# The third weight block of the out projection in buffers of its own, split before the projection begins

## The chip, the cores and the metric

The kernel runs on one core of one Trainium2 chip. The metric is device time of one execution, in microseconds, as the median of several runs. Five engines work beside each other: TensorE (PE) multiplies, VectorE (DVE), ScalarE (ACT) and GpSimd (POOL) do the elementwise work, SyncE (SP) issues the weight loads. They wait for each other by semaphores only, and each does its own instructions in the order in which they were written.

## The reference

Two decoder layers over 512 tokens of width 1024. Each layer mixes tokens (layer 0 by a gated linear unit, layer 1 by an attention with forgetting), adds cross-attention into 256 memory tokens, multiplies the joined heads by an output matrix (the out projection), adds the residual and normalises, then does a squared-ReLU MLP. All of it is float32.

```python
for layer in range(DEPTH):
    if layer < N_A_LAYERS:
        mix = chunked_sgu(zu, zv, a_w_s[layer], a_b_s[layer])   # gate
    else:
        mix = fox_attention(q, k_sh, v_sh, logcum)              # attention
    mo = memory_attention(qm, mk, mv)
    y = jnp.concatenate([mix, mo], axis=-1) @ w_o[layer]        # out projection
    x = layer_norm(DN_ALPHA * x + y, ln_g[layer, 0], ln_b[layer, 0])
    x = layer_norm(DN_ALPHA * x + sq_relu_mlp(x, w_up[layer], w_down[layer]),
                   ln_g[layer, 1], ln_b[layer, 1])
```

## The kernel before

Activations lie transposed in SBUF, 8 tiles of 128 features by 512 tokens. Every weight matrix is streamed in blocks of 128 output features (1024 x 128, 512 KB). A float32 product is made of three products of the faster type fp32r: both operands are split into a high part (a cast copy, `hi`) and the rest (`lo = whole - hi`), and TensorE adds hi*hi, hi*lo and lo*hi. So a block goes through four stations:

1. SP loads it into one of two places of `w_raw` as soon as the block two before it is split (`load`, waits for `w_split`).
2. ScalarE copies it into `w_hi`: `prepare` on that engine, the copy is line 1066. It waits until the block has landed and until TensorE no longer needs the place (`space(b)`, a count of `w_used`).
3. VectorE subtracts, `w_lo = w_raw - w_hi`: `prepare` on that engine, the subtraction is line 1462 (the helper `rest`).
4. TensorE runs 24 products (line 513) into one of two PSUM banks `proj`.

`w_hi` and `w_lo` have two places each, taken in turn, so that a block can in general be split only when TensorE has finished the block two before it. A few blocks have places of their own (`SPLIT_UNITS`, `split_hi` and `split_lo`), and for them `space` asks for nothing; for those in `EARLY_UNITS` it asks for three blocks before instead of the usual one.

The blocks are numbered through the program. The out projection has eight: 18 to 25 in layer 0 and 114 to 121 in layer 1. In the prediction, block 1 to block 8 stand for these in either layer. The first two are multiplied in pieces while the gate or the last attention step still runs (`out_start`), and are finished after it. Block 3 and block 4 are multiplied whole (512 tokens); for blocks 5 to 8 TensorE does the first 256 tokens of each, then the second 256. Blocks 7 and 8 are `SPLIT_UNITS`. Odd blocks use bank `proj0`, even ones `proj1`, and a bank is free when VectorE has added it into the residual `x32`.

What stands around that, in `out_projection`:

- VectorE adds the residual of blocks 1 and 2 (line 1665), takes a shift for the layer norm (line 1709, from a TensorE product `shift_sum` that stands after 15 of the 24 products of block 3), subtracts it from both tiles (line 1672), and for blocks 3 and 4 does a subtraction of the shift (line 1678) and an add of the bank (line 1684). For blocks 5 to 8 the subtraction is line 1691 and the add of half the tokens line 1702. Between these stand the calls of `prepare`.
- ScalarE squares each finished tile (lines 1203 and 1210) between its own calls of `prepare`.
- GpSimd sums the tiles and their squares (lines 2054 and 2064).
- TensorE reads these sums (`layer_sums`, line 813) after the first halves of blocks 5 to 8. All later work of the layer stands behind that.

The order on each engine is written out by hand; nothing is scheduled by a program.

## Time and profile before

| | us |
|---|---|
| median of 3 runs | 1207.45 |
| lowest and highest | 1206.73, 1207.56 |
| the profiled execution, its own time | 1207.21 |
| its span in the trace | 1205.5 |
| TensorE matmuls busy | 1161.2 (96%) |
| VectorE busy | 632.7 (52%) |
| ScalarE busy | 491.2 (41%) |
| GpSimd busy | 129.3 (11%) |

About 1.7 us of the profiled execution lie outside its span. TensorE is busy almost throughout, so time can be won only where it waits, or where it runs at a lower clock. The out projection of layer 0 lies at 160 to 205 us of the span, that of layer 1 at 794 to 839 us.

### The profile page before, as it was taken

The page shows a single profiled execution, that of the slowest core. Times are in us where ns is not written, and L with a number is a line of the kernel's source. Part 1 is how long each engine was busy: PE and PEld are TensorE (multiplying, and loading weights), DVE is VectorE, ACT ScalarE, POOL GpSimd, SP SyncE. Part 2 cuts the span into 40 slices and gives each one's busy share as a digit, 9 for nine tenths or more (in the row PEclk, how much of TensorE's full clock was granted, in tenths as well). Part 3 has the DMA queues.
Part 4 walks back from the last instruction along what each step waited for, and adds up shares of the span by engine and source line. Part 5 has one row for each costly group of instructions (what it writes and reads, how often), then busy time and mean ns, then how long its engine had stood idle before and what let it go on. Part 6 is the DMA issues. An engine that isn't in the chain of part 4 may idle for free.

```text
span 1205.5 us, 16763 instructions
## 1 busy us (share of the span) xinstructions
PE 1161.2 (96%) x5888; PEld 976.6 (81%) x5888; DVE 632.7 (52%) x1032; ACT 491.2 (41%) x852; POOL 129.3 (11%) x156
## 2 busy tenths in 40 slices
PE   5998999999999999999998999999999999999997
PEld 5777779888888888789877888878888888888886
DVE  4477766644332445345576777866544323445226
ACT  4445535634211333224665555635543212334120
POOL 2300025100000000023300000026200000000000
PEclk9999999999999999999998999999999999999999
DMA  7422122333323333332311122212333333333332
GB/s 219 134 70 71 53 90 86 88 89 103 105 87 104 88 101 91 105 88 73 86 35 53 54 70 62 60 53 84 93 104 90 102 104 87 88 98 93 105 105 87
DMA packets 185590, 107.22 MB, mean 89 GB/s; under 512 B 4482, under 2 KB 180162, under 8 KB 185540
## 3 DMA queue, kind: packets, MB, share of 16 engines
q1 hardware_dynamic: 180112, 99.36, 28.5%
q10 hardware_dynamic: 5428, 7.18, 1.9%
q8 instruction: 32, 0.52, 0.2%
q14 instruction: 18, 0.15, 0.0%
HBM read 104.43 MB, written 2.10 MB: 88 GB/s over the span
## 4 chain that ended last, share of the span: by engine, by line
PE 74%; DVE 4%; ACT 4%; issue 3%; POOL 1%; DMA 0%; DVEq 0%; ACTq 0%; POOLq 0%; SPq 0%
PE proj L513 59%; PE pv L513 3%; PE sc L513 2%; PE proj L846 2%; PE pv L846 2%; PE tr L846 2%; PE sc L846 2%; PE tr L561 1%; DVE w_lo L1462 1%; ACT w_hi L1066 1%; ACT x L1232 1%; ACT x_hi L1234 1%; POOL total L2054 0%; DVE split_lo L1462 0%; POOL total L2064 0%
## 5 line engine op out<-in xcount | busy, mean ns | idle before, releaser
L1462 DVE TENSOR_TENSOR w_lo<-w_raw,w_hi 128x1024 fp32r<-128x1024 f32 x173 | 219.6, 1270 | 172.3 <-ACT w_hi L1066 124.2
L513 PE MATMUL proj<-x_hi,w_hi 128*128 128x512 f32 (+1 forms) x768 | 300.5, 393 | 1.9 <-ACT relu L1097 1.0
L513 PE MATMUL proj<-x_hi,w_lo 128*128 128x512 f32 (+1 forms) x768 | 295.9, 386 | 0.0
L513 PE MATMUL proj<-x_lo,w_hi 128*128 128x512 f32 (+1 forms) x768 | 289.8, 384 | 0.0
L1066 ACT CAST w_hi<-w_raw 128x1024 fp32r<-128x1024 f32 x160 | 166.9, 1044 | 168.6 <-PE proj L513 166.9
L513 PEld LDWEIGHTS proj<-x_hi,w_hi 128*128 128x128 f32 x768 | 146.1, 190 | 28.9 <-ACT x_hi L1234 2.2
L513 PEld LDWEIGHTS proj<-x_hi,w_lo 128*128 128x128 f32 x768 | 145.8, 190 | 29.2
L513 PEld LDWEIGHTS proj<-x_lo,w_hi 128*128 128x128 f32 x768 | 143.1, 189 | 25.7
L513 PE MATMUL proj<-h_hi,w_hi 128*128 128x512 f32 (+1 forms) x384 | 146.4, 381 | 2.5 <-DVE w_lo L1462 2.5
L513 PE MATMUL proj<-h_lo,w_hi 128*128 128x512 f32 (+1 forms) x384 | 146.0, 380 | 0.0
L513 PE MATMUL proj<-h_hi,w_lo 128*128 128x512 f32 (+1 forms) x384 | 146.0, 380 | 0.0
L1755 DVE TENSOR_TENSOR h_raw<-relu 128x512 f32<-128x512 f32 x64 | 44.3, 692 | 157.7 <-ACT relu L1097 157.7
L1097 ACT ACTIVATE relu<-proj 128x512 f32<-128x512 f32 x64 | 38.2, 597 | 196.0 <-PE proj L513 196.0
L513 PEld LDWEIGHTS proj<-h_hi,w_hi 128*128 128x128 f32 x384 | 72.2, 188 | 16.8 <-DVE w_lo L1462 3.1
L513 PEld LDWEIGHTS proj<-h_lo,w_hi 128*128 128x128 f32 x384 | 72.2, 188 | 13.8
L513 PEld LDWEIGHTS proj<-h_hi,w_lo 128*128 128x128 f32 x384 | 72.2, 188 | 13.7
L1129 ACT ACTIVATE probs<-sc,neg_max 128x128 f32<-128x128 f32 (+2 forms) x64 | 33.0, 516 | 55.9 <-DVE neg_max L1521 54.9
L2005 POOL TENSOR_TENSOR x_lo<-x,x_hi 128x256 fp32r<-128x256 f32 (+1 forms) x56 | 48.5, 875 | 58.0 <-ACT x L1230 24.8
L1462 DVE TENSOR_TENSOR h_lo<-h_raw,h_hi 128x512 f32 (+1 forms) x64 | 44.3, 692 | 14.9 <-ACT h_hi L1246 14.4
L2054 POOL TENSOR_TENSOR total<-x 128x512 f32<-128x512 f32 x3 | 4.5, 1499 | 440.9 <-DVE x L1672 440.9
L513 PE MATMUL proj<-mix_hi,w_hi 128*128 128x256 f32 (+1 forms) x128 | 45.8, 358 | 2.5 <-DVE w_lo L1462 2.2
L1665 DVE SCALAR_TENSOR_TENSOR x<-x,proj 128x512 f32 (+1 forms) x22 | 15.1, 687 | 61.0 <-PE proj L513 61.0
(344 smaller groups left out, 1805.4 us busy)
## 6 DMA issues: line engine op xcount, KB each, us to landing
w_raw<-in_w_up SPq DMA_DIRECT2D x64, 512.0 KB, 4.0
w_raw<-in_w_down SPq DMA_DIRECT2D x64, 512.0 KB, 3.6
w_raw<-in_w_o SPq DMA_DIRECT2D x16, 512.0 KB, 3.6
w_raw<-in_a_w_in SPq DMA_DIRECT2D x14, 512.0 KB, 3.8
w_raw<-in_kv_w SPq DMA_DIRECT2D x12, 512.0 KB, 3.9
w_raw<-in_mem_w_kv SPq DMA_DIRECT2D x8, 512.0 KB, 4.9
w_raw<-in_b_w_q SPq DMA_DIRECT2D x8, 512.0 KB, 3.6
x_nat<-in_x ACTq DMA_DIRECT2D x2, 1024.0 KB, 11.4
```

Source lines behind the costliest of these rows:

```text
L513: last = pe.matmul(target, lhs, rhs, start=start and n == 0, stop=stop and n == len(terms) - 1)
L561: last = pe.transpose(tr[t.slot][0:n, at:at + rows], piece, ident[0:rows, 0:rows])
L846: last = pe.matmul(rows_of[t][n][:, :], lhs, rhs, start=False, stop=stop and m == 2, skip_group_check=True)
L1066: act.copy(weights(b)[0], w_raw[:, b.slot]).then_inc(w_hi_ready, 1)
L1097: act.activation(target, proj[g.slot][:, 0:target.shape[-1]], function).then_inc(proj_free[g.slot], 1)
L1129: act.activation(probs[:, u % 2, 0:n], sc[u % 2][:, 0:n], ACT.Exp, bias=neg_max[:, u:u + 1], accum_out=row_sum[:, u:u + 1]).then_inc(exp_d ...
L1232: act.activation(x32[:, k, own], x32[:, k, own], ACT.Identity, **gain).then_inc(fin_ready, 1)
L1234: act.copy(x_hi[:, k, own], x32[:, k, own]).then_inc(x_hi_ready, 1)
L1462: return dve.tensor_tensor(target, whole, hi.bitcast(F32), ALU.subtract)
L1665: dve.scalar_tensor_tensor(out=tile if target is None else target, in0=tile, scalar=ALPHA if first else 1.0, in1=proj[g.slot][:, :], op0=A ...
L1755: dve.tensor_tensor(raw, wide, wide, ALU.mult).then_inc(relu_sq, 1)
L2005: pool.tensor_tensor(x_lo[:, k, own], x32[:, k, own], x_hi[:, k, own].bitcast(F32), ALU.subtract).then_inc(x_ready, 1)
```

## The change

Block 3 of both layers (20 and 116, the new `LEAD_UNITS`) gets buffers of its own, `lead_hi` and `lead_lo`, in the 8 KB of `qm`, the memory queries, which are no longer read by then. Its `prepare` moves ahead: in layer 0 behind the loop of the gate, in layer 1 into the last attention step, on ScalarE and VectorE before the last `attended`. Inside `out_projection` every later `prepare` moves up by one: block 4 stands where block 3 stood, and so on, and the last of them (block 8) stands before the first half of block 5 is squared or added. Block 5 (22, 118) may be split as soon as block 1 is finished.

```diff
-    EARLY_UNITS = [26, 27, 28, 29, 30, 31, 92, 93, 94, 122, 123, 124, 125]
+    LEAD_UNITS = [20, 116]
+    EARLY_UNITS = LEAD_UNITS + [22, 118, 26, 27, 28, 29, 30, 31, 92, 93, 94, 122, 123, 124, 125]
...
+        lead_hi = put("lead_hi", [P, KT, P], F32R, top + 32 * K1)
+        lead_lo = put("lead_lo", [P, KT, P], F32R, top + 36 * K1)
...
+            if b.trip is None and b.base in LEAD_UNITS:
+                return lead_hi[:, :, :], lead_lo[:, :, :]
             return w_hi[:, b.slot], w_lo[:, b.slot]
...
+                if late is not None:
+                    prepare(Pos(LEAD_UNITS[1]))
...
             def out_projection(layer):
                 b, g, n = B_WO[layer], G_WO[layer], 2 * layer
-                prepare(Pos(b + 2))
+                prepare(Pos(b + 3))
                 shift_source(n, g)
-                prepare(Pos(b + 3))
+                prepare(Pos(b + 4))
                 for j in range(4):
                     if j >= 2:
-                        prepare(Pos(b + j + 2))
+                        prepare(Pos(b + j + 3))
                     squares(n, Pos(j), Pos(g + j))
...
                 for j in range(4, KT):
-                    if j < 6:
-                        prepare(Pos(b + j + 2))
+                    if j == 4:
+                        prepare(Pos(b + 7))
                     part_squares(n, j, 0)
...
+            prepare(Pos(LEAD_UNITS[0]))
             act.wait_ge(sgu_ready, 2 * PAIRS)
...
                 for j in range(2):
                     residual(n, Pos(b + j), Pos(g + j), Pos(j))
-                    prepare(Pos(b + j + 2))
+                for j in range(2):
+                    prepare(Pos(b + j + 3))
                 take_shift(n)
                 shift_tiles(n, g)
                 for j in range(2, 4):
                     shifted_residual(n, Pos(b + j), Pos(g + j), Pos(j))
-                    prepare(Pos(b + j + 2))
+                    prepare(Pos(b + j + 3))
...
                 for j in range(4, 6):
                     pre_shift(n, j)
-                    prepare(Pos(b + j + 2))
+                    if j == 4:
+                        prepare(Pos(b + 7))
                     part_residual(n, b + j, j, 0)
```

What this does to the order, first on ScalarE in layer 1, from the end of the last attention step (`pb_hi`, `mix_hi`) to the first square of half a tile. `split_hi20` and `split_hi21` are blocks 7 and 8, `lead_hi` is block 3, `w_hi` the others in turn. Before:

```order
L1081 CAST pb_hi1_110<-tr1 128x4x128
L1145 CAST mix_hi_82<-pv1 64x512
L1066 CAST w_hi_51<-w_raw_54 128x1024
L1214 CAST shift_in_132<-x32_53 128x512
L1066 CAST w_hi_51<-w_raw_54 128x1024
L1203 ACTIVATE square_135<-x32_53 128x512 x2
L1066 CAST w_hi_51<-w_raw_54 128x1024
L1203 ACTIVATE square_135<-x32_53 128x512
L1066 CAST w_hi_51<-w_raw_54 128x1024
L1203 ACTIVATE square_135<-x32_53 128x512
L1066 CAST split_hi20_150<-w_raw_54 128x1024
L1210 ACTIVATE square_135<-x32_53 128x256
```

Of the changed kernel, the same stretch:

```order
L1087 CAST pb_hi1_110<-tr1 128x4x128
L1072 CAST lead_hi_158<-w_raw_54 128x1024
L1151 CAST mix_hi_82<-pv1 64x512
L1072 CAST w_hi_51<-w_raw_54 128x1024
L1222 CAST shift_in_132<-x32_53 128x512
L1072 CAST w_hi_51<-w_raw_54 128x1024
L1211 ACTIVATE square_135<-x32_53 128x512 x2
L1072 CAST w_hi_51<-w_raw_54 128x1024
L1211 ACTIVATE square_135<-x32_53 128x512
L1072 CAST split_hi20_150<-w_raw_54 128x1024
L1211 ACTIVATE square_135<-x32_53 128x512
L1072 CAST split_hi21_151<-w_raw_54 128x1024
```

The copy ahead of the third square was that of block 5 and is now that of block 6, and block 8 is copied ahead of the first half square.

On VectorE in layer 1, from the first add of bank `proj0` after block 3 to the second add of half a tile. Before:

```order
L1684 TENSOR_TENSOR x32_53<-x32_53,proj0 128x512
L1462 TENSOR_TENSOR w_lo_52<-w_raw_54,w_hi_51 128x1024
L1678 SCALAR_TENSOR_TENSOR x32_53<-x32_53,shift_131 128x512
L1684 TENSOR_TENSOR x32_53<-x32_53,proj1 128x512
L1462 TENSOR_TENSOR w_lo_52<-w_raw_54,w_hi_51 128x1024
L1691 SCALAR_TENSOR_TENSOR x32_53<-x32_53,shift_131 128x512
L1462 TENSOR_TENSOR split_lo20_156<-w_raw_54,split_hi20_150 128x1024
L1702 TENSOR_TENSOR x32_53<-x32_53,proj0 128x256
L1691 SCALAR_TENSOR_TENSOR x32_53<-x32_53,shift_131 128x512
L1462 TENSOR_TENSOR split_lo21_157<-w_raw_54,split_hi21_151 128x1024
L1702 TENSOR_TENSOR x32_53<-x32_53,proj1 128x256
```

Of the changed kernel:

```order
L1695 TENSOR_TENSOR x32_53<-x32_53,proj0 128x512
L1471 TENSOR_TENSOR w_lo_52<-w_raw_54,w_hi_51 128x1024
L1689 SCALAR_TENSOR_TENSOR x32_53<-x32_53,shift_131 128x512
L1695 TENSOR_TENSOR x32_53<-x32_53,proj1 128x512
L1471 TENSOR_TENSOR split_lo20_156<-w_raw_54,split_hi20_150 128x1024
L1702 SCALAR_TENSOR_TENSOR x32_53<-x32_53,shift_131 128x512
L1471 TENSOR_TENSOR split_lo21_157<-w_raw_54,split_hi21_151 128x1024
L1713 TENSOR_TENSOR x32_53<-x32_53,proj0 128x256
L1702 SCALAR_TENSOR_TENSOR x32_53<-x32_53,shift_131 128x512
L1713 TENSOR_TENSOR x32_53<-x32_53,proj1 128x256
```

The split between the adds of blocks 3 and 4 was that of block 5 and is that of block 6, and block 8 is split before the first half add instead of before the second.

## Rows read from the trace of the kernel before

**Rows 1.** The page, part 1: each engine's busy us, share and instructions.
```profile
PE 1161.2 (96%) x5888; PEld 976.6 (81%) x5888; DVE 632.7 (52%) x1032; ACT 491.2 (41%) x852; POOL 129.3 (11%) x156
```

**Rows 2.** Timeline, TensorE, layer 0: start, duration, instruction, count, [idle before, releaser].
```profile
163.52 0.39 PE L513 MATMUL proj<-mix_hi,w_lo 128*128 128x512 f32 x1
164.32 0.50 PE L513 MATMUL proj<-mix_hi,w_hi 128*128 128x512 f32 x1 [0.42 <-DVE w_lo L1462]
...
167.86 0.39 PE L513 MATMUL sc<-shift_in,ones_r 128*128 128x512 f32 x1
...
175.81 0.39 PE L513 MATMUL proj<-mix_hi,w_lo 128*128 128x512 f32 x1
...
183.65 0.36 PE L513 MATMUL proj<-mix_hi,split_hi 128*128 128x256 f32 x1 [0.40 <-DVE x L1702]
...
187.36 0.35 PE L513 MATMUL proj<-mix_hi,split_hi 128*128 128x256 f32 x1 [0.61 <-DVE x L1702]
...
191.93 0.60 PE L813 MATMUL sc<-ones_f,total_sq 128*128 128x1 f32 x4
```

**Rows 3.** Timeline, TensorE, layer 1.
```profile
796.11 0.40 PE L513 MATMUL proj<-mix_hi,w_lo 128*128 128x512 f32 x1
798.26 0.50 PE L513 MATMUL proj<-mix_hi,w_hi 128*128 128x512 f32 x1 [1.76 <-DVE w_lo L1462]
...
803.40 0.40 PE L513 MATMUL sc<-shift_in,ones_r 128*128 128x512 f32 x1
...
810.91 0.39 PE L513 MATMUL proj<-mix_hi,w_lo 128*128 128x512 f32 x1
...
818.33 0.36 PE L513 MATMUL proj<-mix_hi,split_hi 128*128 128x256 f32 x1 [1.22 <-DVE x L1702]
...
821.64 0.36 PE L513 MATMUL proj<-mix_hi,split_hi 128*128 128x256 f32 x1 [0.21 <-DVE x L1702]
...
825.26 0.61 PE L813 MATMUL sc<-ones_f,total_sq 128*128 128x1 f32 x4
```

**Rows 4.** By stretches, layer 1: us, busy (x) by engine, PEclk, DMA share, GB/s.
```profile
800.00:801.00 1.00, 1.00 (x4) 0.81 (x3) 0.00 (x0) 0.00 (x0) 0.00 (x0) 0.50 1.07 310
```

**Rows 5.** Timeline, ScalarE, layer 1.
```profile
793.49 0.58 ACT L1145 CAST mix_hi<-pv 64x512 fp32r<-64x512 f32 x1 [2.96 <-PE pv L513]
...
811.40 1.05 ACT L1066 CAST w_hi<-w_raw 128x1024 fp32r<-128x1024 f32 x1 [0.80 <-PE proj L513]
```

**Rows 6.** Timeline, VectorE, layer 1.
```profile
794.10 0.69 DVE L1462 TENSOR_TENSOR mix_lo<-pv,mix_hi 64x512 fp32r<-64x512 f32 x1 [2.85 <-ACT mix_hi L1145]
795.85 0.69 DVE L1665 SCALAR_TENSOR_TENSOR x<-x,proj 128x512 f32<-128x512 f32 x1 [1.05 <-PE proj L513]
...
812.48 1.43 DVE L1462 TENSOR_TENSOR w_lo<-w_raw,w_hi 128x1024 fp32r<-128x1024 f32 x1 [0.38 <-ACT w_hi L1066]
813.84 1.78 DVE L1691 SCALAR_TENSOR_TENSOR x<-x,shift 128x512 f32<-128x512 f32 x1
815.54 2.31 DVE L1462 TENSOR_TENSOR split_lo<-w_raw,split_hi 128x1024 fp32r<-128x1024 f32 x1
```

**Rows 7.** Timeline, GpSimd, layer 1.
```profile
811.54 1.29 POOL L2054 TENSOR_TENSOR total_sq<-total_sq,square 128x512 f32<-128x512 f32 x1
812.80 2.27 POOL L2054 TENSOR_TENSOR total<-total,x 128x512 f32<-128x512 f32 x1
815.03 1.74 POOL L2054 TENSOR_TENSOR total_sq<-total_sq,square 128x512 f32<-128x512 f32 x1
```

**Rows 8.** Timeline, ScalarE then VectorE, layer 0.
```profile
161.96 1.05 ACT L1066 CAST w_hi<-w_raw 128x1024 fp32r<-128x1024 f32 x1 [2.84 <-PE proj L513]
...
161.90 0.69 DVE L1665 SCALAR_TENSOR_TENSOR x<-x,proj 128x512 f32<-128x512 f32 x1 [1.76 <-PE proj L513]
163.04 1.22 DVE L1462 TENSOR_TENSOR w_lo<-w_raw,w_hi 128x1024 fp32r<-128x1024 f32 x1 [0.46 <-ACT w_hi L1066]
```

**Rows 9.** The queues, 155 to 232 us: DMA issues, KB each, median us to landing.
```profile
w_raw<-in_w_o SPq DMA_DIRECT2D x4, 512.0 KB, 3.5
```

More of the change, by code:

```diff
@@ L1648, in pair_step @@
                 turned_probs(s, 7)
+                if late is not None:
+                    prepare(Pos(LEAD_UNITS[1]))
                 if reading:
@@ L1915, in _ @@
                         rest(mix_lo[:, j - 1, cols], gated(j - 1, c), mix_hi[:, j - 1, cols]).then_inc(sgu_ready, 1)
+            prepare(Pos(LEAD_UNITS[0]))
             out_projection(0)
```

## The prediction

> **What bounds the kernel now.** I read the page first: TensorE's matmuls are busy in 96% of the span [rows 1], so only its waits and its clock are left to win, and the change touches one wait in each layer. The timeline of TensorE shows both. In layer 0 the last product of block 2 starts at 163.52 and block 3 begins at 164.32, released by VectorE's split of block 3 [rows 2]. Products of 512 tokens follow each other every 0.23 us, so the loss is 164.32 - 163.75 = 0.6 us. In layer 1 the same place costs 798.26 - 796.34 = 1.9 us [rows 3], and something more: at 800 to 801 the granted clock is 0.50, that is 1.2 instead of 2.4 GHz [rows 4], after an idle stretch of 1.76 us. The 15 products from the start of block 3 to the shift's product take 803.40 - 798.26 = 5.14 us, where layer 0 needs 167.86 - 164.32 = 3.54 us [rows 2, 3]: 1.6 us by the clock.
>
> Then I followed TensorE to its next waits, because what is won here is kept only if nothing behind it is late. Both layers show the same two: the first half of block 7 starts at 183.65 and 818.33, and that of block 8 at 187.36 and 821.64, each released by VectorE's half add (line 1702), which frees the bank [rows 2, 3]. So VectorE is already late there, and the change puts more work in front of exactly that add.
>
> **What is removed and moved: the gain.** The early split must be hidden. In layer 1 ScalarE idles 2.96 us before its last `mix_hi` and VectorE 2.85 us before its last `mix_lo` [rows 5, 6]; a copy takes 1.05 us and a split 1.22 us [rows 8], done one behind the other by about 792.8, before either engine is wanted again. In layer 0 the idle stretches are 2.84 and 1.76 us [rows 8], enough for a copy and a split that ends near 161.4. The issue of the memory load behind the copy in layer 0 waits for VectorE anyway. I cost both at nothing; without the cover each would cost up to 2.3 us.
>
> Layer 0: block 3 follows block 2 at once, **-0.6**. Layer 1: block 3 needs bank `proj0`, which the first residual frees at 795.85 + 0.69 = 796.54 [rows 6]; it starts at 796.6, 1.65 us earlier. With that wait cut to about 0.25 us I expect the clock to stay up, another 1.6 us. So block 4 ends **3.25 us** earlier in layer 1, at 808.05 instead of 811.30.
>
> **What the shift by one costs.** Let t be the end of block 4 on TensorE: 175.81 + 0.39 = 176.20 and 810.91 + 0.39 = 811.30. Block 6 shares its place with block 4, so it cannot be copied before t, in either kernel: ScalarE's copy starts at 811.40, right at t [rows 5]. Before, VectorE had by then done everything for block 4 that needs no bank, and after block 6's split it had one more split (block 7) before the half add. In the changed kernel three things of VectorE now stand behind block 6's split that stood before or beside it: the shift and the add of block 4, and block 8's split. And ScalarE's square of tile 3 now stands behind block 6's copy, which waits for t; GpSimd's second sum of squares waits for that square and comes into the same stretch.
>
> VectorE and GpSimd take turns here. At 812.80 GpSimd's add takes 2.27 us instead of 1.29 while VectorE splits until 813.91; the shift at 813.84 takes 1.78 us and ends at 815.62, 0.55 us after GpSimd's add; the next GpSimd add at 815.03 takes 1.74, and the split at 815.54 takes 2.31, again behind GpSimd's end at 816.77 [rows 6, 7]. So each GpSimd add counts as a turn of 1.15 us for VectorE, a split as 1.15 and a shift or add as 0.6. From t: copy and hand-over 1.2, split of block 6 1.15, GpSimd's turn 1.15, shift 0.6, add 0.6, split of block 7 1.15, turn 1.15, shift 0.6, turn 1.15, split of block 8 1.15, half add 0.4, start 0.1. That is **t + 10.4 us** for the first half of block 7, in place of 818.33 - 811.30 = 7.03 in layer 1 and 183.65 - 176.20 = 7.45 in layer 0 [rows 2, 3]: **+3.4 and +2.95**. Block 8's raw data do not set this: its load is issued after block 6's split at t + 2.4 and lands 3.5 us later [rows 9], copied by t + 7, wanted at t + 8.8.
>
> The Trainium skill, SBUF — State Buffer, section "Who interferes with whom", says that a VectorE tensor-tensor operation with both inputs in SBUF contends with GpSimd's reads, and that whoever is first holds the shared ports for its whole instruction. By that rule the three turns belong into the sum and speak against this change; without it the sum would be t + 6.95, about what both layers show before. The rows above side with the rule.
>
> **What comes back after that.** Block 8 is already split, so VectorE goes from the first half add to the second without the 1.15 us of a split. In layer 0 the second half add is what the rest hangs on (0.61 us of wait at 187.36, then the wait for GpSimd's sums before 191.93 [rows 2]), so all **-1.15** comes back. In layer 1 TensorE becomes the bound: two halves of some 2.95 us with their starts, back to back, instead of 3.31, and GpSimd is done before them, so the second sums product stands some 6.1 us behind block 7 instead of 825.26 - 818.33 = 6.93: **-0.8**.
>
> Sum: layer 0 -0.6 + 2.95 - 1.15 = **+1.2**; layer 1 -3.25 + 3.4 - 0.8 = **-0.65**; together +0.5 us, by the one profiled execution (1207.21, 0.24 below the median, which carries over). The turns were counted at their fullest; where a GpSimd add begins before t, some 0.2 to 0.3 us of a layer fall away. I take **+0.2**, so 1207.65 against the median of 1207.45. What isn't shown in the trace: how many turns really fall into the stretch. With none in either layer block 7 is no later behind t than before, and the case is the first rival's; with one fewer in each it is -2.3 in all. On the other side, one turn more in each is +2.3.
>
> **Rivals.** *The gain stays.* If block 7 is not held up, because VectorE and GpSimd arrange themselves otherwise, the time falls by 0.6 + 3.25 = 3.85, to 1203.6. For it: the splits are all done earlier in absolute time, and VectorE is only 52% busy. Against it: block 6's place keeps its split behind t, and everything is queued behind that. *The clock falls in new places.* The change makes two longer waits in each layer: block 6 waits for bank `proj1` (block 4's add is done at t + 5.1; a half takes 24 products of half the width, 24 x 0.12 = 2.9 us, so block 5 ends at t + 2.9: 2.2 us), and block 7 for 10.4 - 8.1 = 2.3 us. Before, 1.76 us of idle was followed by half clock and a loss of 1.6 us, and the 1.22 us at 818.33 was not: from there to 821.64 are 3.31 us, of which 0.21 idle [rows 3, 4]. [...] A fall on blocks 7 and 8 costs 1.6 us, of which 0.5 hides in the wait for GpSimd in layer 0; if it falls between the two waits, the second absorbs it. Both layers unlucky: +2.7 on my +0.2, 1210.3, slower than before. The Trainium skill, TensorE: Matmul & The Clock Gate, section "The HAM clock gate", says that the throttled state is the default and that activity releases it; by that, longer waits are paid twice, and the trace agrees at 800 us. *The change doesn't do what it says:* block 3 is still late, or the last `mix_lo` comes later by the split that stands before it; then the 1.65 us of layer 1 stay lost, or all 3.25 with the clock, while the cost is paid: 1209.3 to 1210.9. Against it stand the two idle stretches of 2.85 us and more [rows 5, 6].
>
> **How the numbers follow.** A measurement of this kernel can tell about 0.2% (2.4 us) from no change. Given back, near 1207.65: 0.70, its own range 1205.3 (a turn fewer in each layer) to 1209.3 (a fall of the clock in one). The gain stays: 0.13, at 1203.6. Clock falls in both: 0.12, three quarters of it above +2.4. Not as said: 0.05, half of it above. Faster is 0.13 and 0.02 of the first case; slower is 0.09, 0.02 and 0.01 of the first case; the rest is the same. The range 1205.0 to 1209.9 leaves out the two outer cases, nearly.
>
> **What would show it.** Right: block 3 follows block 2 within 0.3 us in both layers; clock 1.00 through block 3 of layer 1; t 3.2 us earlier in layer 1 and 0.6 in layer 0; block 7 starts at t + 10 to t + 10.5 in both, with a new wait of block 6 for line 1695's add; the sums of layer 0 are later by about 1 us and those of layer 1 earlier by less than 1.2. Wrong: block 7 at t + 7 to 8 (the gain stays), or stretches at clock 0.50 on blocks 7 and 8 or on the sums.

## The result, and the profile after

| | us |
|---|---|
| changed kernel, median of 22 runs | 1209.26 |
| kernel before, median of 22 runs beside them (1204.61 to 1209.71) | 1207.23 |
| ratio, with its 95% interval | 1.0020 (1.0012 to 1.0027) |
| profiled execution of the changed kernel, its own time | 1208.62 |
| its span | 1206.9 |

The medians differ by 2.03 us, which is 0.17%, and the ratio is 0.20% above one, with an interval that doesn't reach 1.0000. The forecast was 1207.65, near no change, with 1205.0 to 1209.9 as its range. One of the 22 runs took 4067.59 us and is left out of the reading, as is one of 1924.23 us among the runs beside the experiments. The other 21 lie between 1206.45 and 1210.36, with a median of 1209.05. So the runs of one kernel scatter by 4 to 5 us, more than nearly every effect here, and the medians need many of them.

The timeline of TensorE, layer 0, of the changed kernel answers to [rows 2] (start, duration, instruction, count, [idle before, releaser]):

```profile
163.56 0.39 PE L519 MATMUL proj<-mix_hi,w_lo 128*128 128x512 f32 x1
163.79 0.39 PE L519 MATMUL proj<-mix_hi,lead_hi 128*128 128x512 f32 x1
...
175.17 0.39 PE L519 MATMUL proj<-mix_hi,w_lo 128*128 128x512 f32 x1
...
180.53 0.35 PE L519 MATMUL proj<-mix_hi,w_hi 128*128 128x256 f32 x1 [1.19 <-DVE x L1695]
...
185.92 0.35 PE L519 MATMUL proj<-mix_hi,split_hi 128*128 128x256 f32 x1 [1.84 <-DVE x L1713]
...
192.51 0.61 PE L819 MATMUL sc<-ones_f,total 128*128 128x1 f32 x4 [0.62 <-POOL total L2078]
193.20 0.60 PE L819 MATMUL sc<-ones_f,total_sq 128*128 128x1 f32 x4
```

And layer 1, which answers to [rows 3]:

```profile
799.19 0.40 PE L519 MATMUL proj<-mix_hi,w_lo 128*128 128x512 f32 x1
799.76 0.47 PE L519 MATMUL proj<-mix_hi,lead_hi 128*128 128x512 f32 x1 [0.18 <-DVE x L1676]
803.24 0.39 PE L519 MATMUL sc<-shift_in,ones_r 128*128 128x512 f32 x1
...
810.72 0.39 PE L519 MATMUL proj<-mix_hi,w_lo 128*128 128x512 f32 x1
...
816.05 0.36 PE L519 MATMUL proj<-mix_hi,w_hi 128*128 128x256 f32 x1 [2.07 <-DVE x L1695]
...
821.43 0.35 PE L519 MATMUL proj<-mix_hi,split_hi 128*128 128x256 f32 x1 [0.78 <-DVE x L1713]
...
827.62 0.58 PE L819 MATMUL sc<-ones_f,total_sq 128*128 128x1 f32 x4
```

Block 3 starts right behind block 2 in layer 0, and 0.57 us after block 2's last product in layer 1, where it took 2.15. Behind that stand the two waits that the prediction named: block 6 for the add of line 1695 (1.19 and 2.07 us), block 7 for the half add of line 1713 (1.84 and 0.78 us). With t for the end of block 4, block 7 starts at 185.92 - 175.56 = t + 10.36 and at 821.43 - 811.11 = t + 10.32; before it was 7.45 and 7.03.

The granted clock is the third column from the right in the view by stretches (length, busy us and count of TensorE, its weight loads, VectorE, ScalarE, GpSimd, granted clock, DMA share, GB/s). In the changed kernel:

```profile
196.00:199.00 3.00, 3.00 (x15) 3.00 (x16) 0.49 (x3) 0.29 (x1) 0.00 (x0) 0.52 0.00 0
...
800.00:801.00 1.00, 1.00 (x6) 0.80 (x6) 0.55 (x2) 1.00 (x2) 0.00 (x0) 1.00 0.00 0
...
817.00:820.00 3.00, 3.00 (x16) 3.00 (x16) 3.00 (x3) 1.04 (x1) 2.87 (x2) 0.50 0.45 129
```

At 800 the clock is now full, where [rows 4] has half. But there are two new stretches at 1.2 GHz: one behind the sums of layer 0 (in the kernel before, the row of this stretch has 1.00 and 28 products instead of 15), one on block 6 of layer 1.

To see where the time goes I cut each layer's stretch, from block 2's last product to the first product of 512 tokens of the MLP, at t, at block 7 and at the second product of the sums. (The times are starts of rows like those above, and t is the last row of block 4 plus 0.39. "To MLP" means that product of 512 tokens throughout; the MLP's products of 256 tokens begin before it, at 213.90 and 838.64 in the kernel before.)

| us | layer 0: to t | to block 7 | to sums | to MLP | layer 1: to t | to block 7 | to sums | to MLP |
|---|---|---|---|---|---|---|---|---|
| before | 12.68 | 7.45 | 8.28 | 35.57 | 15.19 | 7.03 | 6.93 | 32.68 |
| changed | 12.00 | 10.36 | 7.28 | 37.09 | 11.92 | 10.32 | 6.19 | 31.74 |
| difference | -0.68 | +2.91 | -1.00 | +1.52 | -3.27 | +3.29 | -0.74 | -0.94 |

Up to the sums layer 0 is +1.23 and layer 1 -0.72. Behind the sums there is +1.52 in layer 0, the stretch at half clock, and -0.94 in layer 1, where the kernel before has such a stretch at 844 to 847.5 and the changed one has none. Both layers together are +1.1; the span is 1.4 longer, of which 0.3 lies in the long part between the two projections.

This is one execution of each kernel. For most others the mean granted clock of the whole run is known. It is 0.9908 over the 21 runs of the changed kernel and 0.9924 over 88 runs of the kernel before beside the experiments (means that are good to about 0.0004), while the two profiled executions have 0.992 both. So in its other executions the changed kernel spends more time at half clock than in this trace, and more than the kernel before. By an estimate, 0.0016 of 1207 us is some 4 us more at half clock than before, and up to 2 us of time where no wait takes it in.

### The profile page after: what moved, and what is told of

Same layout as the page of the kernel before. It is cut to its first block, busy times and chain, and to the rows that moved or that the text cites. A ratio compares the mean times of both kernels' runs of the same rounds, so it can differ in the third digit from the quotient of the medians.

```text
span 1206.9 us, 16763 instructions
## 1 busy us (share of the span) xinstructions
PE 1160.6 (96%) x5888; PEld 977.1 (81%) x5888; DVE 632.5 (52%) x1032; ACT 491.5 (41%) x852; POOL 128.1 (11%) x156
## 4 chain that ended last, share of the span: by engine, by line
PE 74%; DVE 5%; ACT 4%; issue 2%; DMA 1%; POOL 1%; DVEq 0%; ACTq 0%; SPq 0%; POOLq 0%
PE proj L519 59%; PE pv L519 3%; PE sc L519 2%; PE proj L852 2%; PE pv L852 2%; PE tr L852 2%; PE sc L852 2%; PE tr L567 1%; DVE w_lo L1471 1%; ACT w_hi L1072 1%; ACT x L1240 1%; DVE split_lo L1471 1%; ACT x_hi L1242 1%; DMA w_raw<-in_w_o 0%; ACT probs L1131 0%
## 5 line engine op out<-in xcount | busy, mean ns | idle before, releaser
L1471 DVE TENSOR_TENSOR w_lo<-w_raw,w_hi 128x1024 fp32r<-128x1024 f32 x171 | 217.0, 1269 | 183.0 <-ACT w_hi L1072 134.7
L1254 ACT ACTIVATE h_hi<-relu 128x512 f32 (+1 forms) x64 | 40.5, 633 | 7.4
```

The costliest lines, as they stand in the source:

```text
L1254: act.activation(h_hi[:, bass.ds(tile.at(), 1), :], relu[:, tile.slot:tile.slot + 1, :], ACT.Square).then_inc(h_hi_ready, 1)
L1471: return dve.tensor_tensor(target, whole, hi.bitcast(F32), ALU.subtract)
```

## The experiments

Times are given against runs of the kernel before on the same chip, which had medians of 1205.93 to 1206.42.

**One part alone.** First the early split of block 3 alone, with every later split where it stood:

```diff
-                prepare(Pos(b + 3))
                 shift_source(n, g)
-                prepare(Pos(b + 4))
+                prepare(Pos(b + 3))
...
-                        prepare(Pos(b + j + 3))
+                        prepare(Pos(b + j + 2))
...
-                    if j == 4:
-                        prepare(Pos(b + 7))
+                    if j < 6:
+                        prepare(Pos(b + j + 2))
```

(the same on VectorE, where block 4 is split behind both residuals).

> Block 3 keeps its own buffers and its early split in both layers, but every later split of the out projection stands where it stood before the change. Theory A, the queue: what costs is the work put ahead of the add that frees the bank for block 7, so here block 7 starts 7.0 to 7.5 us behind the end of block 4 (as before) instead of 10.3, both gains stay, and the time is 0.6 + 3.25 = 3.85 us below the kernel before (3.0 to 4.5). Theory B, the place: the early split itself, or the load that follows it, costs as much as it wins; then the time is within 1 us of the kernel before. Theory C, the clock: the half clock falls in by chance of phase as often as before; then the gain is 2.2 us, without the 1.6 us of the clock.

Measured: 1205.68, ratio 0.9992 (0.9981 to 1.0003). In the trace t comes after 11.96 and 11.97 us in the two layers, block 7 at t + 7.45 and t + 7.04, the sums after another 8.29 and 6.93. So both gains of the early split are there in full, -0.72 and -3.22, and the queue behind t is the old one to 0.01 us: the cost behind t is the moved splits' alone. Yet the median fell by 0.25 us, where 3.85 were expected. In layer 0 the stretch from the sums to the MLP takes 38.65 instead of 35.57: the clock is at half there for 6.8 us. This is the row of the stretch; before, it has 1.00 and 29 products:

```profile
193.00:196.00 3.00, 3.00 (x16) 3.00 (x16) 0.75 (x5) 0.30 (x1) 0.00 (x0) 0.50 0.00 0
```

Then the change in one layer only, here layer 0 (with 116 and 1 for layer 1; the places where the code asks for the layer again are left out):

```diff
-    LEAD_UNITS = [20, 116]
+    LEAD_UNITS = [20]
+    LEAD_LAYER = 0
...
-                prepare(Pos(b + 3))
+                up = 3 if layer == LEAD_LAYER else 2
+                prepare(Pos(b + up))
                 shift_source(n, g)
-                prepare(Pos(b + 4))
+                prepare(Pos(b + up + 1))
```

> The whole change, in layer 0 only. Theory A: +1.2 us (gain 0.6, block 7 later behind block 4 by 2.95, 1.15 back). Theory C: the longer waits of blocks 6 and 7 bring half clock into the stretch of the sums in most executions, another 1.6 us: +2.8. The changed kernel's trace has it so: the first product behind the layer's normalisation starts 2.8 us later.

> The whole change, in layer 1 only. Theory A: -0.65 us. If the half clock falls between the waits of blocks 6 and 7 it hides, as in the changed kernel's trace (-1.6 there from the end of block 2 to the MLP); if it falls later, it costs up to 1.6: +1. The sum of this one and that of layer 0 alone should give the +2.0 of the full change; if it doesn't, the layers act on each other.

Measured: layer 0 alone 1208.62, ratio 1.0019 (1.0008 to 1.0030); layer 1 alone 1205.86, 1.0009 (0.9998 to 1.0020). In the layer that is changed block 7 starts at t + 10.35 and t + 10.34, in the other one at 7.04 and 7.45 as before. Layer 0 has 38.14 from the sums to the MLP (half clock again), and layer 1 alone shows 35.54 there. Layer 1 alone needs 7.68 us from block 7 to the sums, where the changed kernel needs 6.19: the stretch at half clock begins 0.4 us behind the start of block 7 there, where no wait takes it in, and not on block 6. Most of the loss thus sits in layer 0. Of layer 1 the trace says +1.1 us, and -0.7 if the 1.5 us of this stretch and 0.3 behind the sums are taken off, and its median can't be told from no change. The two ratios add up to 1.0028, against 1.0020 for the change in both layers. That is within their intervals, so nothing shows that the layers act on each other.

**What stands in the queue.** The changed kernel with ScalarE's square of tile 3 ahead of block 6's copy, no longer behind it, and, apart from that, the changed kernel with VectorE's add of block 4 ahead of block 6's split:

```diff
                 for j in range(4):
-                    if j >= 2:
+                    if j >= 3:
                         prepare(Pos(b + j + 3))
                     squares(n, Pos(j), Pos(g + j))
+                    if j == 2:
+                        prepare(Pos(b + 5))
```

```diff
                 for j in range(2, 4):
                     shifted_residual(n, Pos(b + j), Pos(g + j), Pos(j))
+                for j in range(2, 4):
                     prepare(Pos(b + j + 3))
```

> The changed kernel, but ScalarE squares tile 3 ahead of its copy of block 6, so that GpSimd's second sum of squares is over before the end of block 4. If GpSimd's turn in that stretch is one term of 1.15 us of the sum, block 7 starts 9.2 us behind the end of block 4 instead of 10.3 in layer 1. If VectorE's own queue is the bound and GpSimd merely fills gaps, it stays at 10.3.

> The changed kernel, but VectorE takes the shift and the add of block 4 ahead of the split of block 6. The add is then over 0.8 us after the end of block 4: block 6 starts without a wait, 2.9 us behind it instead of 4.9. Block 7 by the sum: 10.4 less 1.2 for the two operations, so 9.1 to 9.3 us; if GpSimd's turns simply follow, only 0.6 of it is saved.

Measured: one run each, 1207.58 and 1207.50, beside one of before of 1206.16. With the square first, block 7 starts at t + 9.86 in layer 0 and t + 9.25 in layer 1. With the add first it is 9.92 and 9.01, and block 6 no longer waits in layer 1. So 1.07 and 1.31 us go in layer 1, about the turn of 1.15 and the two operations of 0.6 that the two edits take away, and only 0.50 and 0.44 us in layer 0. With one run each, these two are read from their traces alone. What is late next is a thing that my sum had set aside: block 8's raw data. ScalarE, with the square first, in layer 1 (t is 809.80) and layer 0 (t is 174.75):

```profile
815.86 1.05 ACT L1072 CAST split_hi<-w_raw 128x1024 fp32r<-128x1024 f32 x1 [1.67 <-DMA w_raw<-in_w_o]
```
```profile
180.96 1.05 ACT L1072 CAST split_hi<-w_raw 128x1024 fp32r<-128x1024 f32 x1 [0.75 <-DMA w_raw<-in_w_o]
```

The copy waits for the data until about t + 6.1: block 6 is split by t + 2.4, and the load issued then takes 3.6 us or so. As long as block 6 is split behind t and block 8's split stands before the half add, copy, split, half add and start give about t + 9 (an estimate from these rows), however empty VectorE is. In the changed kernel itself this copy starts at 817.33, t + 6.22, and VectorE takes up block 8's split only 0.24 us after the copy has handed over.

**Away with the cause.** What keeps block 6 behind t is its place. In the changed kernel the places of block 3 are free again once block 3 is done, so block 6 can take them and be split before t:

```diff
+    SIXTH_UNITS = [23, 119]
...
-            if b.trip is None and b.base in LEAD_UNITS:
+            if b.trip is None and b.base in LEAD_UNITS + SIXTH_UNITS:
                 return lead_hi[:, :, :], lead_lo[:, :, :]
...
+            if b.trip is None and b.base in SIXTH_UNITS:
+                return b.base - 2
```

> The changed kernel, with block 6 put into the same new buffers once block 3 is done with them, so that its split no longer waits for block 4. Theory A: behind the end of block 4 VectorE has only one add, one split, one shift, one split and the half add, so block 7 starts at about 5.8 us behind it, without a wait; -3.85 us as when the order is kept, and the waits of blocks 7 and 8 (1.2 + 0.2 in layer 1, 0.4 + 0.6 in layer 0) shrink too: -4.5 to -6 us. Theory B: within 1 us of the kernel before. Theory C: with waits under 1 us the half clock of the out projections is gone, and the spread of the runs is smaller.

Measured: 1203.59, ratio 0.9981 (0.9971 to 0.9992), faster than before and than the changed kernel, but by 2.3 us where 4.5 to 6 were expected. Block 7 starts at t + 9.08 in layer 0 and t + 7.04 in layer 1. In layer 1 that is 1.2 us above what was expected: VectorE's splits of blocks 7 and 8, and the shift between them, still wait for GpSimd adds. These are its rows (t is 809.35); the split of block 8 takes 2.31 us, of which 1.1 are GpSimd's:

```profile
810.06 1.92 DVE L1474 TENSOR_TENSOR split_lo<-w_raw,split_hi 128x1024 fp32r<-128x1024 f32 x1
811.91 1.78 DVE L1705 SCALAR_TENSOR_TENSOR x<-x,shift 128x512 f32<-128x512 f32 x1
813.61 2.31 DVE L1474 TENSOR_TENSOR split_lo<-w_raw,split_hi 128x1024 fp32r<-128x1024 f32 x1
815.84 0.41 DVE L1716 TENSOR_TENSOR x<-x,proj 128x256 f32<-128x256 f32 x1
```

In layer 0 (t is 174.85) VectorE idles until t + 1.1 for a piece of the memory tokens that ScalarE copies late, behind a square that itself waited for GpSimd:

```profile
175.99 0.69 DVE L1474 TENSOR_TENSOR memt_lo<-tr,memt_hi 128x512 fp32r<-128x512 f32 x1 [2.52 <-ACT memt_hi L1090]
```

The same kernel with block 8's split behind the first half add:

```diff
                     pre_shift(n, j)
+                    part_residual(n, b + j, j, 0)
                     if j == 4:
                         prepare(Pos(b + 7))
-                    part_residual(n, b + j, j, 0)
```

> Block 6 in the new buffers too (as in the run before), and VectorE's split of block 8 put back behind the first half add. Queue theory: in layer 1 the half add moves from 15.84 to about 13.6 us on that trace's scale, block 7 starts right behind block 6 at about 5.8 us after the end of block 4 instead of 7.04, block 8 right behind block 7; in layer 0 block 7 starts at about 6.9 us instead of 9.1. Against the run before -1.2 in layer 1, less what GpSimd's sums take back, and -1.5 in layer 0: -3.5 to -5 us against the kernel before. If the sums by GpSimd are what the end hangs on, blocks 7 and 8 come earlier but the sums don't, and the time stays at -2.3.

Measured: 1203.05, ratio 0.9972 (0.9957 to 0.9986), 3.3 us below before, where 3.5 to 5 were expected. Block 7 starts at t + 7.11 and t + 5.59: the half add no longer waits for the split, and in layer 1 no wait above 0.2 us is left on TensorE between block 3 and the sums:

```profile
812.41 1.78 DVE L1705 SCALAR_TENSOR_TENSOR x<-x,shift 128x512 f32<-128x512 f32 x1
814.22 0.42 DVE L1716 TENSOR_TENSOR x<-x,proj 128x256 f32<-128x256 f32 x1
814.56 1.86 DVE L1474 TENSOR_TENSOR split_lo<-w_raw,split_hi 128x1024 fp32r<-128x1024 f32 x1
```

**The clock.** Two kernels add spare TensorE products of 512 tokens, whose results nothing reads, where TensorE would wait, and touch nothing else. They stand behind block 2 of layer 1 in the kernel before (eight of them), and in the waits of blocks 6 and 7 and before block 8 and the sums in the changed kernel (`fill(n)` issues n of them):

```diff
+                for _ in range((0, 8)[layer]):
+                    pe.matmul(pv[1][:, :], ones_r[:, :], mix_hi[:, 0], start=True, stop=True)
                 project(b.plus(2), g.plus(2), mix_hi, mix_lo, order=out_order, parts=(0, 5))
```

```diff
                 for j in range(4, KT):
+                    fill(({5: 4, 6: 7, 8: 2}, {5: 8, 6: 9})[layer].get(j, 0))
                     part(j, 0)
...
+                fill(({5: 4, 6: 7, 8: 2}, {5: 8, 6: 9})[layer].get(8, 0))
```

> The kernel before, with 8 extra products (as above, result not read) ahead of block 3 in layer 1 alone, where TensorE waits 1.76 us. Clock theory: block 3 runs at clock 1.00, and where the kernel before had half clock there it saves 1.6 us: -1.6 if it has it in every execution, less if only in some. Without the clock's part: 0 to +0.3.

> The changed kernel, with extra products of 512 tokens (operands that are there, a PSUM bank that is free, result not read) put into TensorE's new waits: 4 and 7 of them ahead of blocks 6 and 7 in layer 0 and 2 ahead of the sums, 8 and 9 ahead of blocks 6 and 7 in layer 1. They fit into the waits, so they delay nothing by themselves. Queue theory alone (+0.5 from the turns, clock irrelevant): no faster than the changed kernel, or slower by the extra work, 0 to +1. Clock theory (the rest of the +2.0 is half clock behind the longer waits): about 1.6 us below the changed kernel, that is +0 to +0.7 against the kernel before, no half clock between blocks 5 of layer 0 and its second sums, and none on blocks 6 and 7 of layer 1.

Measured: the kernel before with its wait filled, 1206.86, ratio 1.0011 (0.9998 to 1.0024). Its trace has the clock at 1.00 through block 3, and t comes 1.61 us sooner, as the term of 1.6 us said. But the median doesn't follow. In the trace the stretch at half clock between the sums and the MLP of layer 1 is 6.8 us long instead of 3.4, but the way there is only 0.34 us longer (33.02 instead of 32.68), so this doesn't take back the 1.61 us. The mean granted clock of its 12 runs is 0.9923, that of the kernel before beside them 0.9925: taken over all executions, filling this wait gained no clock, and where the half clock fell instead is not shown. The changed kernel, filled: 1207.67, 1.0012 (1.0002 to 1.0022), with a mean clock of 0.9940 instead of 0.9908; block 7 at t + 10.38 in both layers, clock 1.00 at both new places, sums to MLP 35.56 in layer 0. The 1.5 us there are the clock's and not the queue's. In layer 1 nothing is won up to the sums: the half clock on block 6 had ended inside block 7's wait.

The last question was what brings the half clock to the sums of layer 0. In the traces so far, all seven kernels without spare products whose layer 0 is changed have it, and none of the three with layer 0 as it was. I took the early split alone, and either filled its waits at blocks 7, 8 and the sums, or put five spare products (1.15 us) ahead of block 3, which brings everything behind it back to about its old time and leaves the waits as they are:

```diff
                 for j in range(4, KT):
+                    fill(({6: 1, 7: 2, 8: 3}, {})[layer].get(j, 0))
                     part(j, 0)
```

```diff
+                for _ in range((5, 0)[layer]):
+                    pe.matmul(pv[1][:, :], ones_r[:, :], mix_hi[:, 0], start=True, stop=True)
                 project(b.plus(2), g.plus(2), mix_hi, mix_lo, order=out_order, parts=(0, 5))
```

> The kernel with the early split of block 3 alone (every later split where it stood), and in the out projection of layer 0 six spare TensorE products of 512 tokens whose results nothing reads: one before the first half of block 7, two before that of block 8, three before the sums product, each set about as long as the wait there (0.39, 0.61 and 0.78 us in that kernel's profile without them). Theory A (the early split's gain is eaten by the half clock at the sums of layer 0, and what lets the clock fall there is TensorE's waits at blocks 7 and 8 and at the sums): clock 1.00 through the sums, last product of block 2 to the MLP's first product 66.35 - 3.1 = 63.3 us, median some 3 us below the 1205.68 of the kernel without them, about 0.9975 of before. Theory B (the clock falls there for another reason, such as work further back): half clock again at about 191 to 198, 66.3 us or more, median no better than 1205.7.

> The kernel with the early split of block 3 alone, and in layer 0 five spare TensorE products of 512 tokens between block 2 and block 3 (1.15 us), so that block 3 starts at about 164.4, near the 164.32 of the kernel before, and everything behind it has the order, the waits and nearly the time of the kernel before. Theory A (whether the sums of layer 0 fall to half clock depends on when they come, since kernel before and the early split alone have the same waits from the end of block 4 on, and only the second showed half clock): no half clock at the sums, last product of block 2 to the MLP's first product about 64.3 us instead of 66.35, and a median about 2 us below that of the early split alone although TensorE does 1.15 us more. Theory B (the early split itself brings it about): half clock at the sums, 67.5 us, median 1 us above 1205.7.

Measured: filled, 1204.65, ratio 0.9981 (0.9970 to 0.9992); later by five products, 1204.51, 0.9982 (0.9971 to 0.9994). The row of 193 to 196 us, first filled, then later:

```profile
193.00:196.00 3.00, 3.00 (x27) 3.00 (x28) 1.25 (x7) 0.30 (x1) 0.00 (x0) 1.00 0.00 0
```
```profile
193.00:196.00 3.00, 3.00 (x28) 3.00 (x28) 0.73 (x5) 0.61 (x2) 0.00 (x0) 1.00 0.00 0
```

In both the full clock is back, with 35.56 us from the sums to the MLP, and the way from block 2 to the MLP is 63.29 and 64.39 us where the early split alone has 66.35. The second is the telling one: its waits at blocks 7, 8 and the sums are 0.40, 0.61 and 0.79 us, those of the early split alone 0.39, 0.61 and 0.78. The same waits met half clock when they came at one time and full clock when they came 1.7 us later, of which 1.15 are the spare products and 0.6 lie before them. 1.15 us of useless work made the trace of layer 0 shorter by 1.96 us. These are single executions, and another one of either kernel might fare otherwise; but the mean granted clock of all runs goes the same way, 0.9919 for the early split alone, 0.9936 filled and 0.9935 later (12, 11 and 12 runs, on two chips on which the kernel before has 0.9925 and 0.9923). By the medians both kernels are 1.0 to 1.2 us below the early split alone, where 2 and 3 were expected; the intervals of the three overlap, so that part rests on the traces and the clock. That it is the time of coming, and not the five products themselves just ahead of block 3, is argued from the waits and not shown by itself.

The same fill on the fastest kernel so far, one product before block 8 and three before the sums of layer 0:

```diff
                 for j in range(4, KT):
+                    fill(({7: 1, 8: 3}, {})[layer].get(j, 0))
                     part(j, 0)
```

> The kernel with block 6 early and block 8's split behind the first half add, and in layer 0 four spare TensorE products: one before the first half of block 8 (0.32 us of wait in that kernel's profile), three before the sums product (0.79 us). Theory A (waits around the sums let the clock fall): no half clock at the sums of layer 0, last product of block 2 to the MLP's first product 65.77 - 3.1 = 62.7 us, median about 1200.0 to 1200.5 where the kernel without them had 1203.05. Theory B (another reason, or the clock falls later instead, as when the wait before block 3 of layer 1 was filled in the kernel before): the half clock stays or moves, median 1202.5 to 1203.5.

Measured: 1201.21, ratio 0.9956 (0.9941 to 0.9971) over 7 runs, the fastest of all, with a mean clock of 0.9936 instead of 0.9918. From block 2 to the MLP layer 0 takes 62.60 us; without the fill it was 65.77. The interval overlaps that of the kernel without the fill. Block 6 early, block 8's split behind the half add and four spare products make the change worth -0.44% instead of +0.20%.

## Why the prediction was right, and where not

- **The early split is hidden and the wait goes.** Held. Block 3 starts 0.23 us behind block 2's last product in layer 0. In layer 1 it starts 0.57 us behind it and waits 0.18 us for the residual of line 1676. The way to t is 0.68 and 3.27 us shorter, where 0.6 and 3.25 were put down. The 1.6 us of clock are among them: from block 3 to the shift's product it is 803.24 - 799.76 = 3.48 us instead of 5.14.
- **Block 7 at t + 10.4.** The number held in both layers, 10.36 and 10.32; step by step it held in layer 1 alone. VectorE in layer 1, which answers to [rows 6], from t = 811.11:

```profile
812.28 1.22 DVE L1471 TENSOR_TENSOR w_lo<-w_raw,w_hi 128x1024 fp32r<-128x1024 f32 x1 [5.27 <-ACT w_hi L1072]
813.43 1.76 DVE L1689 SCALAR_TENSOR_TENSOR x<-x,shift 128x512 f32<-128x512 f32 x1
815.22 0.69 DVE L1695 TENSOR_TENSOR x<-x,proj 128x512 f32<-128x512 f32 x1
815.83 1.22 DVE L1471 TENSOR_TENSOR split_lo<-w_raw,split_hi 128x1024 fp32r<-128x1024 f32 x1
816.96 1.77 DVE L1702 SCALAR_TENSOR_TENSOR x<-x,shift 128x512 f32<-128x512 f32 x1
818.65 2.30 DVE L1471 TENSOR_TENSOR split_lo<-w_raw,split_hi 128x1024 fp32r<-128x1024 f32 x1
820.88 0.41 DVE L1713 TENSOR_TENSOR x<-x,proj 128x256 f32<-128x256 f32 x1
```

  Copy and hand-over 1.17, split 1.15, shift with a turn 1.79, add 0.61, split 1.13, shift with a turn 1.69, split with a turn 2.23, half add and start 0.55. The three turns are there: two shifts of 0.6 and a split of 1.15 take 1.1 us more each. GpSimd's adds beside them start at 812.86, 815.99 and 818.15. What I allowed for fewer turns (the step from +0.5 to +0.2) didn't come. In the rival's text block 4's add is done at t + 5.1, where the terms of the sum give t + 4.7; block 6, which waits for it, started at t + 4.97 and t + 4.94.

  In layer 0 the same total is luck. VectorE there, from t = 175.56:

```profile
176.73 1.22 DVE L1471 TENSOR_TENSOR w_lo<-w_raw,w_hi 128x1024 fp32r<-128x1024 f32 x1 [4.06 <-ACT w_hi L1072]
177.88 0.69 DVE L1471 TENSOR_TENSOR memt_lo<-tr,memt_hi 128x512 fp32r<-128x512 f32 x1
178.49 1.18 DVE L1689 SCALAR_TENSOR_TENSOR x<-x,shift 128x512 f32<-128x512 f32 x1
179.70 0.69 DVE L1695 TENSOR_TENSOR x<-x,proj 128x512 f32<-128x512 f32 x1
180.30 1.22 DVE L1471 TENSOR_TENSOR split_lo<-w_raw,split_hi 128x1024 fp32r<-128x1024 f32 x1
181.56 0.69 DVE L1471 TENSOR_TENSOR memt_lo<-tr,memt_hi 128x512 fp32r<-128x512 f32 x1
182.16 1.06 DVE L1702 SCALAR_TENSOR_TENSOR x<-x,shift 128x512 f32<-128x512 f32 x1
183.15 2.29 DVE L1471 TENSOR_TENSOR split_lo<-w_raw,split_hi 128x1024 fp32r<-128x1024 f32 x1
```

  Two operations of the memory tokens (`memt_lo`, from the PSUM tile `tr`) stand in the queue and take 0.6 us each; the sum has no term for them. GpSimd's adds start at 177.31, 180.46 and 182.63, and the first two run on during a `memt_lo`, which is not slowed (0.69 us). So the two shifts behind it lose only about 0.5 and 0.4 us, and the split 1.1: some 2.1 us for the three turns instead of 3.45. The missing 1.2 and the surplus of about 1.3 cancel.
- **What comes back.** Held: 1.00 in layer 0 where 1.15 was put down, 0.74 in layer 1 where it was 0.8. Up to the sums this makes +1.23 and -0.72 against +1.2 and -0.65.
- **Block 8's raw data do not set this.** True here by 0.2 us only (in layer 1 VectorE took up the split at t + 7.54, and the sum wanted it at t + 8.8 because it put the last turn ahead of it), and wrong as soon as a turn is gone: the sum had no term for the next bound, at about t + 9.
- **The clock falls in new places.** This is the rival that came half true, and it is the step that failed. I forecast that the clock would stay up apart from this rival, and priced it as a loss on blocks 7 and 8; the sum has no term for the stretch behind the sums. It fell in two places: on block 6 of layer 1, where the next wait took it in, as the rival's text says; and behind the sums of layer 0, where nothing takes it in and which costs 1.5 us. I had named the sums only in the list of what would show me wrong. I had judged the risk by the length of single waits, 1.76 us against 1.22, and that tells nothing here. The early split alone fell to half clock after waits of 0.39, 0.61 and 0.78 us, and the same waits 1.7 us later kept the full clock. The trace of the kernel before could have warned me: its stretch at 844 comes with no wait above 0.44 us in the 20 us ahead of it. And with the square first, a wait of 2.28 us at 819.05 is followed by 23 us at full clock. The row of the kernel before, then that of the square first:

```profile
844.00:847.50 3.50, 3.50 (x19) 3.50 (x18) 1.56 (x5) 1.38 (x2) 0.34 (x1) 0.51 0.90 271
```
```profile
819.00:842.00 23.00, 22.82 (x189) 22.54 (x190) 14.22 (x34) 12.68 (x25) 14.26 (x17) 1.00 0.16 47
```

  The Trainium skill, TensorE: Matmul & The Clock Gate, Part 1: The HAM clock gate (the "warmup" mystery), says that the watching is free-running, so that the same kernel pays differently with its phase. By that, when the work comes counts too, and not only how long it waits; the pair of traces agrees, with 38.65 against 35.56 us behind the same waits.
- **The sum.** The queue's +0.5 us was measured at +0.51. With the clock behind the sums, +1.52 - 0.94, the trace has +1.1, and the medians +2.0. Of what lies between the trace and the medians the runs show the direction: the profiled execution was 0.64 us below its kernel's median, and the mean granted clock of the other runs is lower, 0.9908 against 0.992 in the trace. Where in the kernel they meet the half clock no run here shows. The measured median lies inside the range because the range was drawn up to the price of a fall of the clock, though on other blocks than the one where it came; the queue alone would have given +0.5.

## What to carry to other kernels

A split or copy that is moved to an earlier place moves the whole queue behind it. Take the instruction that still has to wait for something fixed (here block 6's copy, for the end of block 4) and list what now stands behind it: that list, with a turn for each GpSimd operation in it, gave the loss in layer 1 to 0.1 us. In layer 0 it left out two operations and still came out, so list every operation of the engine and not only those of the change. The cure was not to undo the move but to take the fixed thing away (block 6 into the places that block 3 leaves), and to keep the add that frees a bank ahead of a split that nobody waits for. On a kernel whose TensorE is 96% busy, a gain of some microseconds can be undone by stretches at half clock far behind the edit, so compare the granted clock stage by stage before blaming the edit; four spare products in short waits ahead of such a stage took 3.2 us off it in the trace, and 0.16% off the ratio.

## What the runs showed of the hardware

- A granted clock of half speed came behind waits of under 0.8 us each, and with the same waits shifted by 1.7 us it did not come. After a wait of 2.28 us it did not come for 23 us (the square first, layer 1). Spare products that filled those waits kept it away in four kernels of four in the stretch where they stood.
- Filling one wait need not raise the clock on the whole: in the kernel before, the filled wait in layer 1 brought t 1.6 us forward in the trace, but the next stretch at half clock was 6.8 us long instead of 3.4, and the mean granted clock of the runs stayed at 0.992. Where waits between block 5 and the sums were filled it rose, from 0.9908 to 0.9940, from 0.9919 to 0.9936 and from 0.9918 to 0.9936.
- A VectorE operation with both inputs in SBUF that meets the start of a GpSimd add takes 1.1 us longer (1.76 for a shift of 0.68, 2.30 for a split of 1.22), and less where the add has run for a while (1.92 for a split that begins 0.45 us into one, 1.18 and 1.06 for the shifts of layer 0). One with an input in PSUM kept its 0.69 us beside such an add (`memt_lo` at 177.88). Which operation pays changes from kernel to kernel.
